# A token shift made tile by tile, context sums moved forward, and expert blocks split among the gather's copies

## The chip, the cores and the metric

The kernel runs on one core of a Trainium2 chip. Its time is the device time of one execution in microseconds (us), and the metric is the median of several runs. TensorE is PE in the profile, VectorE is DVE, ScalarE is ACT, GpSimd is POOL and SyncE is SP.

## The reference

256 tokens of width 1024 pass through two blocks of two layers each. The first block has a pooling and neighbourhood-attention layer and then an RWKV layer; it also carries a context sequence of 256 tokens (CTX) beside the latent one (X). The second block has a differential and a sparse attention layer, each followed by a mixture of 16 experts in 4 groups. The parts that matter here:

```python
def centred_shift(x):
    prev = jnp.pad(x[:, :-1], ((0, 0), (1, 0), (0, 0)))
    nxt = jnp.pad(x[:, 1:], ((0, 0), (0, 1), (0, 0)))
    return 0.5 * (prev + nxt) - x

xx = centred_shift(h)
mix = lambda j: h + xx * mu[j]
r = mix(0) @ wr        # latent tokens only
k = mix(2) @ wk        # context and latent tokens; also w, v, a, g from mixes 1, 3, 4, 5
```

The shift pads with a zero token at either end, so the sum at an edge is the one neighbour there is, which the program copies. In an expert layer each token takes one group of four experts by its router logits, and in it the two best experts with weights from the logits. An expert computes `(silu(x @ w_gate) * (x @ w_up)) @ w_down`.

## The kernel before

**Order.** Each engine has one program written out by hand, and it runs in that order. `step(...)` raises a semaphore and may name an event; `after(event)` gives the value to wait for. Tiles hold 128 features by 256 tokens, so the width of 1024 is eight tiles, k = 0 to 7. All 318 weight blocks (1 MB each) come through a ring of four slots (`N_SLOTS`), in the order of use. SP issues block j when block j - 4 is marked "used". `take_bank` hands out the PSUM banks in turn from a given list, and PE waits there until the last holder's result is taken.

**Mixes** (`mixes_vector`, from line 1784; `features_tensor`, 1882; `features_scalar`, 1944). ACT adds the shift of the modulation to the eight tiles of X (`shifted_scalar`, line 855). DVE then runs `shifted(X)`: the sum of both neighbours for all tiles (L1791), two edge copies (L1792, L1793), and 0.5 x sum - h (L1795). The mixes of `r` follow, one per k (L1804). PE multiplies them by wr, tile by tile (g = 0 to 7, each over all k, L941, two tiles per weight block). Behind g = 3 come the sums of squares of the context (L787), for which DVE and ACT have meanwhile finished the context's residual; and then g = 4 to 7. The root of these sums (L811) releases DVE's reciprocal (L818) and scaling (L847), ACT's shift (L855), `shifted(CTX)` and the mixes of `k` over both sequences. In between ACT splits the wk weights into high parts (`wk_high`, L1715) and DVE into low parts (L1720), and ACT copies wr's results out (L1395), tile 7 only after it has rounded all mixes of `k` (`mix_k_high`, L1726). `wk_tensor` (L1744) takes three banks for its first three tiles and walks k over them. Products whose result nobody reads (`unread_products`, L798) fill PE's time ahead of waits: 12 before wr and 3 before wk.

**Experts** (`moe_tensor`, 2857; `moe_vector`, 3018; `moe_scalar`, 3173; both layers). The router's products and transposes are followed by a gather: one-hot matrices times tokens give the inputs of five windows of 128 slots. The eight `pair` products (windows 0 and 1) and the eight times two `rest` products (windows 2 to 4) are copied out of their banks by ACT and DVE (L3184, L3188, L3094, L3098). Then weight block 0 is split into a high part on ACT (`Splits.high`, L507) and a low part on DVE (`Splits.low`, L516), and so on. There are 20 units; unit u does `gate_up(u)` (24 products of 512 columns, L2933 to L2935), `turn(u)` (two transposes, L2946) and `down(u)` (12 products, L2964 to L2966). Units 0 and 1 use the same weights on windows 0 and 1. `gate_up(u + 1)` is issued ahead of `down(u)`, with `turn(u)` between its two halves. Between unit 0's gate_up and unit 1's, PE transposes the places (L2996) and sums the slot weights (L3003, 10 products of 4 columns, 20 records), which wait for the token weights that DVE works out (L3110 to L3118).

## Time and profile before

| | |
|---|---|
| median of 3 runs | 2454.49 us (2449.64 to 2457.53) |
| the profiled execution | 2451.6 us, its span 2449.8 us |
| busy: PE, DVE, ACT | 94%, 69%, 41% of the span |
| mean granted clock of TensorE | 0.976 of full speed |
| read from HBM | 343.96 MB, 141 GB/s over the span |

The span is from the first instruction to the last. A busy PE is one with a product in its pipeline. The idle time given with a row is that of its engine just before it, with the instruction that ended it. An fp32 product shows as two records, so "x24" of such products is 12 of them; products of rounded (fp32r) operands show as one.

### The profile page before, as it was taken

To read this page: it belongs to the slowest core of one execution; us is meant where nothing else is said; L and a number is where in the kernel's file an instruction comes from. 1 tells how busy PE (TensorE), PEld (TensorE's weight loads), DVE (VectorE), ACT (ScalarE), POOL (GpSimd) and SP (SyncE) were. 2 spreads that over 40 slices of the span, in tenths; PEclk is the share of its full clock that TensorE was granted. 3 is DMA by queue.
4 is the path that set the end of the run, shared out by engine and by line. 5 is a ranking of instruction groups with operands and counts; after the bars stand their busy time and mean duration, and the time that the engine had idled before them with its cause. 6 is when DMAs were issued, how large, how long until landed. Compare 5 with 4: busy or idle time off the path is not lost.

```text
span 2449.8 us, 46605 instructions
## 1 busy us (share of the span) xinstructions
PE 2294.3 (94%) x20260; PEld 1907.2 (78%) x20260; DVE 1698.9 (69%) x3082; ACT 1006.5 (41%) x1763; POOL 44.7 (2%) x53
## 2 busy tenths in 40 slices
PE   7988999999999999999999989998999999898997
PEld 6864578888868678998897789895677878676786
DVE  7988698867746367887763887765455866646576
ACT  2244242332323225544422553344345655544464
POOL 1000000000000000000000000020000011000000
PEclk9999999999999989999999999999989999998999
DMA  8512437656512000000003577540055853104484
GB/s 341 206 52 86 155 139 274 242 205 245 218 64 105 31 1 3 4 3 3 12 4 124 211 267 295 224 172 18 1 195 216 338 203 113 70 1 157 169 335 180
DMA packets 47308, 348.00 MB, mean 142 GB/s; under 512 B 5264, under 2 KB 5280, under 8 KB 5760
## 3 DMA queue, kind: packets, MB, share of 16 engines
q1 hardware_dynamic: 45936, 334.52, 36.7%
q0 software_dynamic: 1168, 10.51, 1.1%
q8 instruction: 159, 2.61, 0.4%
q14 instruction: 45, 0.37, 0.0%
HBM read 343.96 MB, written 1.05 MB: 141 GB/s over the span
## 4 chain that ended last, share of the span: by engine, by line
PE 75%; DVE 17%; ACT 6%; issue 1%; DMA 1%; DVEq 0%; ACTq 0%; POOLq 0%
PE banks L538 25%; PE banks L2071 7%; PE banks L941 6%; PE banks L2933 3%; PE banks L2934 3%; PE banks L2935 3%; PE banks L1930 2%; DVE arena L617 2%; PE banks L787 2%; PE banks L1744 2%; PE banks L636 2%; PE banks L2148 2%; PE banks L2964 2%; PE banks L2966 2%; PE banks L2965 2%
## 5 line engine op out<-in xcount | busy, mean ns | idle before, releaser
L617 DVE SCALAR_TENSOR_TENSOR arena<-weight_slots,silu_c,arena 128x256 f32<-128x256 f32 x776 | 314.9, 479 | 0.0
L516 DVE TENSOR_TENSOR moe_w_low<-weight_slots,moe_w_high 128x2048 fp32r<-128x2048 f32 x96 | 217.9, 2288 | 69.0 <-ACT moe_w_high L507 68.1
L507 ACT ACTIVATE mlp_w_high<-weight_slots 128x2048 fp32r<-128x2048 f32 x64 | 122.3, 1911 | 180.8 <-PE banks L538 115.6
L507 ACT ACTIVATE moe_w_high<-weight_slots 128x2048 fp32r<-128x2048 f32 x96 | 181.1, 1910 | 22.9 <-PE banks L2966 19.7
L516 DVE TENSOR_TENSOR mlp_w_low<-weight_slots,mlp_w_high 128x2048 fp32r<-128x2048 f32 x64 | 146.4, 2287 | 48.7 <-ACT mlp_w_high L507 48.6
L941 PE MATMUL banks<-arena,weight_slots 128*128 128x256 f32 (+1 forms) x640 | 171.9, 425 | 2.8 <-DVE arena L1804 1.4
L2071 PE MATMUL banks<-weight_slots,arena 64*64 64x64 f32 (+1 forms) x3648 | 147.0, 223 | 18.9 <-ACT arena L2091 13.3
L2071 PEld LDWEIGHTS banks<-weight_slots,arena 64*64 64x64 f32 x3648 | 138.9, 134 | 27.2 <-ACT arena L2091 15.2
L941 PEld LDWEIGHTS banks<-arena,weight_slots 128*128 128x128 f32 x640 | 122.0, 192 | 47.0 <-issue 33.6
L2933 PE MATMUL banks<-moe_w_high,slots_x 128*128 128x512 f32 x320 | 131.9, 412 | 3.2 <-DVE moe_w_low L516 3.2
L2934 PE MATMUL banks<-moe_w_low,slots_x 128*128 128x512 f32 x320 | 128.2, 401 | 0.0
L2935 PE MATMUL banks<-moe_w_high,slots_x 128*128 128x512 f32 x320 | 128.1, 400 | 0.0
L2299 ACT ACTIVATE weight_slots<-banks 128x512 f32<-128x512 f32 x80 | 46.9, 595 | 120.0 <-DVE weight_slots L2478 94.1
L2148 PE MATMUL banks<-weight_slots 64*64 64x64 f32 x2560 | 83.6, 220 | 9.2 <-DVE weight_slots L2515 9.2
L2148 PEld LDWEIGHTS banks<-weight_slots 64*64 64x64 f32 x2560 | 78.9, 135 | 11.2 <-DVE weight_slots L2515 11.2
L2515 DVE TENSOR_TENSOR weight_slots<-banks,constants 128x512 f32<-128x512 f32 x80 | 54.2, 688 | 40.4 <-PE banks L2071 40.4
L614 DVE TENSOR_SCALAR arena<-weight_slots,silu_c 128x256 f32<-128x256 f32 x184 | 56.2, 348 | 32.9 <-PE banks L636 19.1
L1181 ACT ACTIVATE arena<-arena 128x256 f32<-128x256 f32 (+2 forms) x128 | 62.2, 488 | 36.7 <-DVE arena L1125 36.5
L2071 PE MATMUL banks<-arena 64*64 64x64 f32 (+1 forms) x1600 | 77.1, 226 | 0.0
L787 PE MATMUL banks<-arena,constants 128*128 128x256 f32 (+1 forms) x224 | 69.2, 435 | 6.4 <-ACT arena L839 6.4
L2933 PEld LDWEIGHTS banks<-moe_w_high,slots_x 128*128 128x128 f32 x320 | 61.3, 191 | 17.9 <-DVE moe_w_low L516 4.2
L2071 PEld LDWEIGHTS banks<-arena 64*64 64x64 f32 x1600 | 74.1, 134 | 0.3 <-issue 0.3
(428 smaller groups left out, 5109.3 us busy)
## 6 DMA issues: line engine op xcount, KB each, us to landing
weight_slots<-weights SPq DMA_DIRECT2D x318, 1024.0 KB, 4.8
arena<-small POOLq DMA_DIRECT2D x1, 2560.0 KB, 9.0
arena<-x_t POOLq DMA_DIRECT2D x1, 2048.0 KB, 9.6
arena<-bias POOLq DMA_DIRECT2D x1, 2048.0 KB, 8.4
constants<-consts POOLq DMA_DIRECT2D x1, 1410.0 KB, 14.6
out_t<-arena SPq DMA_DIRECT2D x1, 1024.0 KB, 3.9
parameters<-params POOLq DMA_DIRECT2D x1, 763.0 KB, 18.4
arena<-pool_inv POOLq DMA_DIRECT2D x1, 512.0 KB, 9.6
```

What stands on the lines that cost most here:

```text
L507: nc.scalar.activation(self.pair(j)[0], slot(j, 0, SLOT), ACT.Copy).then_inc(*act.step("high", j))
L516: nc.vector.tensor_tensor(self.pair(j)[1], slot(j, 0, SLOT), self.pair(j)[0], ALU.subtract).then_inc(*v.step("used", j))
L538: ins = nc.tensor.matmul(out, self.pair(j)[part][:, at:at + P], x(k), start=start and n == 0 and k == 0, stop=stop and n == 2 and k == til ...
L617: nc.vector.scalar_tensor_tensor(a_, w, c, a_, ALU.mult, ALU.add).then_inc(*v.step())
L787: ins = nc.tensor.matmul(psum(SUMS_BANK[segs[-1]], 0, len(segs) * SEQ), cn("ones"), squares_of(key, segs, k), start=(k == 0), stop=(k == K ...
L941: ins = nc.tensor.matmul(psum(b, 0, w), slot(j, k, 256, i * P, P), moving(k), start=(k == 0), stop=(k == KT - 1))
L1181: nc.scalar.activation(S[:, u % N, c:c + w], S[:, u % N, c:c + w], ACT.Exp, bias=M[:, u % N, 3 + j:4 + j], accum_out=M[:, u % N, 6 + j:7 + ...
L2071: ins = nc.tensor.matmul(psum(b, n * width, width, r), lhs, rhs, start=(i == 0), stop=(i == len(ts) - 1))
L2148: ins = nc.tensor.matmul(psum(b, p * 64, 64, r), Z[r, p, :], XI[r, p, :], start=False, stop=True, skip_group_check=True)
L2933: nc.tensor.matmul(psum(b), x_hi, wh, start=(k == 0), stop=False)
L2934: nc.tensor.matmul(psum(b), x_hi, wl, start=False, stop=False)
L2935: ins = nc.tensor.matmul(psum(b), x_lo, wh, start=False, stop=(k == KT - 1))
```

## The change

The diff changes three things. The token shift and the first mix that needs it are made tile by tile, in a pipeline on DVE over three tiles. PE's first four wr tiles advance together, k by k, and the context's sums follow them; 8 unread products stand before wr where there were 12. In both expert layers the gather's banks are fixed in an order (`GATHER_BANKS`), blocks 0 and 1 are split among the copies of the rest, the five unread products ahead of the first unit go, the slot weights are summed between the two halves of the second unit, and the places are transposed behind it; ACT copies them behind that unit's SiLU. Blocks 2 and 3 are split at other places of the same lists too.

```diff
--- before.py
+++ after.py
@@ -1785,24 +1785,41 @@
 
...
 
-            def shifted(seg):
-                v.wait_ge(*after("h", "n1_1", KT - 1, seg))
-                H, S = HT[:, seg], XX[:, seg]
-                nc.vector.tensor_tensor(S[:, :, 1:255], H[:, :, 0:254], H[:, :, 2:256], ALU.add).then_inc(*v.step())
-                nc.vector.tensor_copy(S[:, :, 0:1], H[:, :, 1:2]).then_inc(*v.step())
-                nc.vector.tensor_copy(S[:, :, 255:256], H[:, :, 254:255]).then_inc(*v.step())
-                v.wait_ge(*v.own)
-                nc.vector.scalar_tensor_tensor(S, S, 0.5, H, ALU.mult, ALU.subtract).then_inc(*v.step())
-                v.wait_ge(*v.own)
-
-            shifted(X)
+            def mixed_tile(i, k):
+                n, mu, segs = MIX_ORDER[i]
+                sg = seg_of(segs)
+                nc.vector.scalar_tensor_tensor(MIX[i % 2][:, sg, k, :], XX[:, sg, k, :],
+                                               pr("mu", mu * KT + k, 1), HT[:, sg, k, :], ALU.mult, ALU.add).then_inc(*v.step("mix", n, k))
+
+            def shifted_and_mixed(seg, i):
+
+                summed, centred = {}, {}
+                for k in range(KT + 2):
+                    if k < KT:
+                        v.wait_ge(*after("h", "n1_1", k, seg))
+                        H, S = HT[:, seg, k, :], XX[:, seg, k, :]
+                        nc.vector.tensor_tensor(S[:, 1:255], H[:, 0:254], H[:, 2:256], ALU.add).then_inc(*v.step())
+                        nc.vector.tensor_copy(S[:, 0:256:255], H[:, 1:255:253]).then_inc(*v.step())
+                        summed[k] = v.own
+                    if 1 <= k <= KT:
+                        v.wait_ge(*summed[k - 1])
+                        S = XX[:, seg, k - 1, :]
+                        nc.vector.scalar_tensor_tensor(S, S, 0.5, HT[:, seg, k - 1, :], ALU.mult, ALU.subtract).then_inc(*v.step())
+                        centred[k - 1] = v.own
+                    if k >= 2:
+                        v.wait_ge(*centred[k - 2])
+                        mixed_tile(i, k - 2)
+
             for i, (n, mu, segs) in enumerate(MIX_ORDER):
...
                     v.wait_ge(*after(*MIX_END[MIX_ORDER[i - 2][0]]))
-                sg = seg_of(segs)
-                for k in range(KT):
-                    nc.vector.scalar_tensor_tensor(MIX[i % 2][:, sg, k, :], XX[:, sg, k, :],
-                                                   pr("mu", mu * KT + k, 1), HT[:, sg, k, :], ALU.mult, ALU.add).then_inc(*v.step("mix", n, k))
+                if n == "r":
+                    shifted_and_mixed(X, i)
+                elif n == "k":
+                    shifted_and_mixed(CTX, i)
+                else:
+                    for k in range(KT):
+                        mixed_tile(i, k)
                 if n == "r":
...
                     inverse_root_vector(v, "y_x02", CTX)
@@ -1812,7 +1829,6 @@
                     inverse_root_vector(v, "n1_1", CTX)
...
                     v.stage("mixes")
-                    shifted(CTX)
                 if n == "k":
...
                     mix_k_low(v)
@@ -1881,12 +1897,38 @@
 
...
             mv = lambda i, segs: (lambda k: MIX[i % 2][:, seg_of(segs), k, :])
-            def context_sums(g):
-                if g == 3:
-                    x_sums_tensor(pe, "n1_1", [CTX])
-                    pe.stage("project_wr")
-            project_tensor(pe, "wr", "wr", lambda k: MIX[0][:, X, k, :], lambda k: [("mix", "r", k)], [X], "project_wr",
-                           [0, 1, 2, 3, 4, 6], context_sums)
+            pe.stage("project_wr")
+            WR_BANKS, blocks = [0, 1, 2, 3, 4, 6], {}
+
+            def wr_part(g, k):
+                return nc.tensor.matmul(psum(bank_of(("wr", g)), 0, SEQ), slot(blocks[g // 2], k, 256, g % 2 * P, P),
+                                        MIX[0][:, X, k, :], start=(k == 0), stop=(k == KT - 1))
+
+            def wr_done(ins, g):
+                ins.then_inc(*pe.step("wr", g))
+                if g % 2:
+                    pe.mark("used", blocks[g // 2])
+
+
+            for n in range(2):
+                blocks[n] = next_block(pe, "wr")
+            for g in range(4):
+                take_bank(pe, ("wr", g), WR_BANKS)
+            for k in range(KT):
+                pe.wait_ge(*after("mix", "r", k))
+                for g in range(4):
+                    ins = wr_part(g, k)
+                    if k == KT - 1:
+                        wr_done(ins, g)
+            x_sums_tensor(pe, "n1_1", [CTX])
+            pe.stage("project_wr")
+            for g in range(4, KT):
+                if g % 2 == 0:
+                    blocks[g // 2] = next_block(pe, "wr")
+                take_bank(pe, ("wr", g), WR_BANKS)
+                for k in range(KT):
+                    ins = wr_part(g, k)
+                wr_done(ins, g)
             wk_tensor(pe)
...
                 pe.stage("low_rank")
@@ -2854,6 +2896,8 @@
         def y_banks(w):
...
 
+        GATHER_BANKS = [6, 7, 4, 5, 0, 2, 1, 3]
+
         def moe_tensor(pe, l):
...
             start = block_of[f"moe{l}"][0]
@@ -2895,7 +2939,7 @@
 
...
             for k in range(KT):
-                b = take_bank(pe, ("pair", l, k), range(8))
+                b = take_bank(pe, ("pair", l, k), [GATHER_BANKS[k]])
                 for part in range(2):
...
                         pe.wait_ge(*after("token_low", l, 2 * t + k // 4))
@@ -2905,7 +2949,7 @@
             pe.wait_ge(*after("places", l, 1))
...
                 for part in range(2):
-                    b = take_bank(pe, ("rest", l, k, part), range(8))
+                    b = take_bank(pe, ("rest", l, k, part), [GATHER_BANKS[(2 * k + part) % 8]])
                     for t in range(2):
...
                                                PLACES_R[:, t, SEQ:WINDOWS * P], start=(t == 0), stop=(t == 1))
@@ -2987,24 +3031,31 @@
                 if w < WINDOWS - 1:
...
 
-            unread_products(pe, 5, bank_state["next"] % 8)
+            def slot_weights():
+                b = take_bank(pe, ("slot_weights", l), range(6))
+                pe.wait_ge(*after("token_weights", l))
+                for w in range(WINDOWS):
+                    for t in range(2):
+                        ins = nc.tensor.matmul(psum(b, 4 * w, 4), PLACES[:, t, w * P:(w + 1) * P], ROUTE["first"][:, t],
+                                               start=(t == 0), stop=(t == 1))
+                ins.then_inc(*pe.step("slot_weights", l))
+
+            def places_turned():
+                for n in range(3):
+                    b = take_bank(pe, ("places_t", l, n), range(4))
+                    for w in range(2 * n, min(2 * n + 2, WINDOWS)):
+                        for t in range(2):
+                            ins = nc.tensor.transpose(psum(b, (w % 2) * SEQ + t * P, P), PLACES[:, t, w * P:(w + 1) * P],
+                                                      cn("ident"))
+                    ins.then_inc(*pe.step("places_t", l, n))
+
             gate_up(0)
-            for n in range(3):
...
-            ins.then_inc(*pe.step("slot_weights", l))
             for u in range(N_UNITS):
-                if u + 1 < N_UNITS:
+                if u == 0:
+                    gate_up(1, slot_weights)
+                    turn(0)
+                    places_turned()
+                elif u + 1 < N_UNITS:
                     gate_up(u + 1, lambda: turn(u))
...
                     turn(u)
@@ -3097,15 +3148,14 @@
                 v.wait_ge(*after("rest", l, k, 1))
...
                     *v.step("taken", "rest", l, k, 1))
-            MOE[l].low(v, 0)
-            MOE[l].low(v, 1)
+                if k in (1, 4):
+                    MOE[l].low(v, k // 4)
 
...
             tt(R["less2"], R["max2"], R["max1"], ALU.subtract).then_inc(*v.step("top_less", l))
-            MOE[l].low(v, 2)
             v.wait_ge(*after("route_exp", l))
...
             step(nc.vector.reciprocal(R["sum"], R["sum"]))
@@ -3116,6 +3166,7 @@
             step(tt(R["first"], R["first"], four(R["w1"]), ALU.mult))
...
             tt(R["first"], R["first"], R["second"], ALU.add).then_inc(*v.step("token_weights", l))
+            MOE[l].low(v, 2)
             MOE[l].low(v, 3)
...
             nc.vector.tensor_copy(R["weights"], psum(bank_of(("slot_weights", l)), 0, 4 * WINDOWS).rearrange(
@@ -3183,23 +3234,19 @@
                 act.wait_ge(*after("pair", l, k))
...
                                      ACT.Copy).then_inc(*act.step("taken", "pair", l, k))
+            MOE[l].high(act, 0)
             for k in range(KT):
...
                     *act.step("taken", "rest", l, k, 0))
+                if k == 4:
+                    MOE[l].high(act, 1)
             act.wait_ge(*after("group_less", l))
             nc.scalar.activation(R["less"], R["less"], ACT.Exp).then_inc(*act.step())
-            MOE[l].high(act, 0)
-            MOE[l].high(act, 1)
+            MOE[l].high(act, 2)
             act.wait_ge(*after("top_less", l))
             nc.scalar.activation(R["less2"], R["less2"], ACT.Exp).then_inc(*act.step("route_exp", l))
-            MOE[l].high(act, 2)
             load_table(act, ACT.Silu)
-            for n in range(3):
-                act.wait_ge(*after("places_t", l, n))
...
             MOE[l].high(act, 3)
...
             act.stage(f"experts{l}")
@@ -3219,6 +3266,12 @@
                 if u >= 3:
...
                 nc.scalar.activation(SG[:, u % 3], psum(b, 0, SEQ), ACT.Silu).then_inc(*act.step("silu", l, u))
+                if u == 1:
+                    for n in range(3):
+                        act.wait_ge(*after("places_t", l, n))
+                        m = min(2, WINDOWS - 2 * n)
+                        nc.scalar.activation(PLACES_T[:, 2 * n:2 * n + m, :], psum(bank_of(("places_t", l, n)), 0, m * SEQ).rearrange(
+                            "p (a b) -> p a b", b=SEQ), ACT.Copy).then_inc(*act.step("taken", "places_t", l, n))
                 for i in early:
...
                 for y in range(WINDOWS):
@@ -3603,7 +3656,7 @@
             unread_products(pe, 1, 0)
...
             x_sums_tensor(pe, "n1_1", ONE, 5)
-            unread_products(pe, 12, 0)
+            unread_products(pe, 8, 0)
             features_tensor(pe)
...
             readout_tensor(pe)
```

## Rows read from the trace of the kernel before

**Rows 1.** The page: busy shares, the chain by engine, the weight transfers.
```profile
PE 2294.3 (94%) x20260; PEld 1907.2 (78%) x20260; DVE 1698.9 (69%) x3082; ACT 1006.5 (41%) x1763; POOL 44.7 (2%) x53
...
PE 75%; DVE 17%; ACT 6%; issue 1%; DMA 1%; DVEq 0%; ACTq 0%; POOLq 0%
...
weight_slots<-weights SPq DMA_DIRECT2D x318, 1024.0 KB, 4.8
```

**Rows 2.** The chain in order of time, 690 to 860: start, us, what.
```profile
722.77 2.30 DVE arena L1795
...
725.73 14.05 PE banks L941 x64
739.78 3.47 PE banks L787 x16
...
743.27 0.48 ACT arena L811
...
754.22 5.40 DVE arena L1804 x8
...
760.27 0.28 ACT arena L1395
...
760.69 44.38 PE banks L1744 x192
```

**Rows 3.** Timeline of DVE, 700 to 790: start, us, instruction, idle before.
```profile
720.30 2.28 DVE L1791 TENSOR_TENSOR arena<-arena 128x2032 f32<-128x2032 f32 x1 [0.66 <-ACT arena L855]
722.50 0.17 DVE L1792 COPY arena<-arena 128x8 f32<-128x8 f32 x1
...
725.10 3.25 DVE L1804 SCALAR_TENSOR_TENSOR arena<-arena,parameters 128x256 f32<-128x256 f32 x8
```

**Rows 4.** Timeline of PE, 700 to 790.
```profile
713.83 10.46 PE L798 MATMUL banks<-constants 128*128 128x512 f32 x24
...
756.89 2.74 PE L798 MATMUL banks<-constants 128*128 128x512 f32 x6
```

**Rows 5.** Timeline of ACT, 700 to 790.
```profile
737.60 2.00 ACT L1715 ACTIVATE wk_w_high<-weight_slots 128x1024 fp32r<-128x1024 f32 x2 [0.89 <-DMA weight_slots<-weights]
```

**Rows 6.** Timeline of PE, 356 to 380.
```profile
368.77 1.40 PE L538 MATMUL banks<-quarter_low,mlp_w_high 128*128 128x512 f32 x2 [4.84 <-DVE quarter_low L1589]
369.97 2.98 PE L538 MATMUL banks<-quarter_high,mlp_w_high 128*128 128x512 f32 x8
372.78 1.98 PE L538 MATMUL banks<-quarter_high,mlp_w_low 128*128 128x512 f32 x8
```

**Rows 7.** Windows of 2 us: stretch, busy by engine, PEclk, DMA share, GB/s.
```profile
370.00:372.00 2.00, 2.00 (x6) 1.63 (x5) 2.00 (x6) 1.20 (x1) 0.00 (x0) 0.50 0.98 401
```

**Rows 8.** Timeline of PE, 1740 to 1840.
```profile
1787.88 4.45 PE L798 MATMUL banks<-constants 128*128 128x512 f32 x10
...
1802.87 4.43 PE L3003 MATMUL banks<-arena,places 128*128 128x4 f32 x20 [3.42 <-DVE arena L3118]
1807.16 0.77 PE L2933 MATMUL banks<-moe_w_high,slots_x 128*128 128x512 f32 x1
```

**Rows 9.** Windows of 4 us, 1808 to 1816.
```profile
1808.00:1812.00 4.00, 4.00 (x11) 3.03 (x11) 0.10 (x1) 0.00 (x0) 0.00 (x0) 0.50 0.51 215
1812.00:1816.00 4.00, 4.00 (x19) 3.16 (x18) 1.35 (x2) 2.52 (x4) 0.00 (x0) 0.94 0.00 0
```

**Rows 10.** Timeline of ACT, 1740 to 1840.
```profile
1788.21 3.70 ACT L507 ACTIVATE moe_w_high<-weight_slots 128x2048 fp32r<-128x2048 f32 x2
```

**Rows 11.** Timeline of DVE, 1740 to 1840.
```profile
1783.22 5.42 DVE L3098 CAST slots_x<-banks 128x384 fp32r<-128x384 f32 x8
1790.15 4.49 DVE L516 TENSOR_TENSOR moe_w_low<-weight_slots,moe_w_high 128x2048 fp32r<-128x2048 f32 x2 [1.51 <-ACT moe_w_high L507]
...
1796.62 0.15 DVE L3107 TENSOR_TENSOR arena<-arena 128x2 f32<-128x2 f32 x1
```

**Rows 12.** Timeline of SP's queue, 1740 to 1840.
```profile
1775.05 63.42 SPq L432 DMA_DIRECT2D weight_slots<-weights  x13
```

15 lines of the change are left out of this document (removed).

## The prediction

> **What bounds the kernel now.** I began with the page. The busy shares say that TensorE (PE) works in 94% of the span, and the chain that ended last runs through PE for 75% and through VectorE (DVE) for 17% [rows 1]. A single change elsewhere therefore only counts where PE waits, works on something unneeded, or runs at half clock. The diff touches two kinds of places, so I read the chain and the timelines there, and then the windows for the granted clock.
>
> In the mixes, PE waits for the first product of wr. DVE forms the centred shift of all eight tiles in one piece (2.28 us and 2.30 us), and only then the first mix, so PE starts at 725.73 [rows 2, 3]. The 12 unread products (24 records, 10.46 us) before it are cover for that wait [rows 4]. Later the chain leaves PE for the context half: root at 743.27 on ScalarE (ACT), then DVE to 759.62, ACT's rounding of the last mix, ACT's copy of wr's tile 7 at 760.27, and PE's first wk product at 760.69 [rows 2]. The reader is to see that PE isn't the bound at this place: its wr work ended near 757, and three unread products fill the hole [rows 4].
>
> In each expert layer PE first does five unread products (4.45 us), since the first weight block is split only after the gather's copies: ACT from 1788.21, DVE from 1790.15 [rows 8, 10, 11]. Then, after the first unit, it waits 3.42 us for the token weights, works 4.43 us on slot weights, and the next 512-column products run 0.63 us each instead of the 0.39 of full clock [rows 8]. The clock was 0.50 in 1808 to 1812, that is 1.2 GHz, and its mean of 0.94 in the next four puts the return to 2.4 GHz at 1812.5 [rows 9].
>
> **The mixes, step by step.** Per tile the new loop issues a sum of 254 columns (2.28/8 = 0.29, with its start about 0.34), an edge copy (0.17 long, about 0.07 between starts), a centring (0.40) and a mix (0.40 at 256 columns) [rows 3]: 1.2 us. DVE is free at 719.64 (its first sum starts at 720.30 after 0.66 idle). The first mix comes after three sums and copies, two centrings and itself: 3 x 0.41 + 2 x 0.40 + 0.48 = 2.5, so at 722.1. PE starts at 722.2, which is 3.5 us earlier. It needs 14.05/8 = 1.76 us per k [rows 2], more than DVE's 1.2, so it isn't starved. The 8 unread products that remain take 2/3 of 10.46 us and end at 720.9.
>
> DVE ends this loop at 729.2, 0.9 us later than now. The context squares come that much later, and the other wr tiles cover it: PE reaches the context sums at 736.3 and their last at 739.4, the last square is there at 737.1. So wr ends 3.2 us earlier, at 753.9.
>
> This gain doesn't reach wk. First, wr's block 0 now stays in use until k = 7 of tile 1, about 735.4 and not 732.8, since four tiles advance together. A transfer takes 4.8 us from issue [rows 1], so wk's first block lands at 740.2; ACT waits for it today until 737.60 [rows 5]. Behind that wait on ACT are two roundings (2.0 us), two copies and the root of the context sums, at 742.8. The 3.4 us gained by the sums shrink to some 0.4 us. Second, the context loop on DVE costs per tile 0.34 + 0.07 + 0.40 + 0.67 = 1.48 [rows 2, 3], together 11.8 us from the last scaled tile. Now it is 10.8: the first mix at 754.22, less the two large steps, the copies and the same 0.6 of waiting for ACT, puts that tile's end at 748.8, and the last mix ends at 759.6. ACT rounds the last mix, copies wr tile 7, and the third wk tile takes the bank of just that tile. So PE starts wk at 760.69 + 0.9 - 0.35 = 761.3: 0.6 us later. The bounds are -1.0 (if the root is as early as its sums allow and no start is longer) and +1.5.
>
> Third, PE is now idle from 756.6 to 761.3, 4.7 us instead of 1.1. The nearest row is the wait of 4.84 us at 368.77: the first eight products behind it took 2.98 us and the next eight 1.98, at a clock of 0.50 in between, and the two just behind the wait 1.40 [rows 6, 7]. That is 1.0 + 0.5 = 1.5 us; the bounds are 0 (no drop) and 2.6 (as long as the low stretch after the slot weights). I take 1.5. Mixes together: **+2.1 us**. Nothing behind covers it, for PE runs through wk without a wait.
>
> The Trainium skill, "TensorE: Matmul & The Clock Gate", section "Why this matters for your kernels", warns of just such an idle gap between bursts of products, after which the engine is back at half clock. By it the 1.5 us are due; without it the mixes cost 0.6 us. The trace agrees at 368.77.
>
> **An expert layer.** ACT's splitting of block 0 moves ahead of the rest's copies. The block is issued at 1775.05 [rows 12] and lands at 1779.8, so it is no wait: ACT splits at 1782.6 to 1784.5, DVE forms the low part at 1784.5 to 1786.75 (4.49 for two, [rows 11]). DVE's copies of tiles 2 to 4 are queued behind it; PE needs the bank of tile 2's second part at 1786.8 and gets it at 1787.3. ACT's own delay of 1.9 us is covered by its four banks. The gather stretches by 0.5 us (bounds 0 and 2). New banks spare the first gathers a wait for token copies: -0.25. The unread products go: -4.45, and the first unit starts at 1788.4. Its second half needs block 1: ACT 1786.3 to 1788.2, DVE to 1790.5, while PE comes there at 1791.2. Covered.
>
> DVE then copies three rests (5.42/8 is a pace set by PE; alone about 0.47 each), ends them at 1792.0, and needs 2.2 us to the step at 1796.62 of today (12 steps from 1794.6, 0.18 each [rows 11]), so 1794.2; ACT's exponential and nine such steps give token weights at 1796.2. PE is halfway through the second unit at 1796.9, so the wait of 3.42 goes whole; its slack is 0.7 us. The slot weights (4.43) and the transposes cost what they cost, only elsewhere. The transposes' copies on ACT (three, 1.3 us) go behind the second unit's SiLU, where ACT waits for PE anyway, and PE needs them only eight units later.
>
> The clock: today 12 products start at 1807.16 at 1.2 GHz and take 5.1 us (0.427 for 512 columns), where at full clock eight take 1.98 [rows 6] and 12 take 2.9: 2.2 us lost [rows 8, 9]. PE was busy with the 4-column products for 4.43 us, and the clock was still low behind them, so 4.4 us of them between two dense halves may well lower it. The nearest rows are again those at 368.77: I put 1.3 us, bounds 0 and 2.4. Per layer: -4.45 + 0.5 - 0.25 - 3.4 - 2.2 + 1.3 = **-8.5 us**, -17.0 for both; the second layer adds -0.5, since its first gather waits longer for a bank today. Later units move as a whole: PE is their bound, and each split is released by PE's own progress.
>
> Sum: 2.1 - 17.5 = -15.4 us. Against the profiled execution (2451.6 us, span 2449.8) it gives 2436.2; against the median of the three runs, 2454.5, it gives 2439.1. I say **2438.5 us**.
>
> **Rivals.**
> *The clock holds.* The slot weights count as work and wk's gap falls well: then -17.5 - 2.6 - 1.5 = -21.6, 2433. For it: PE issues the slot weights without a pause, unlike in the wait of rows 6; against it: [rows 6, 7, 9]. Chance 0.16.
> *The weight stream takes the lead back.* The first transfer of a layer is issued at 1775.05 either way [rows 12], so if transfers and splits set the end of the layer, both leads are lost and only the mixes' +2.1 stays: 2456.6, no change. For it: a block costs DVE 2.25 us and ACT 1.85 of their time; against it: the chain hardly leaves PE. Chance 0.10.
> *A late token weight.* DVE's chain has 0.7 us of slack; 2 to 3 us more cost 2 per layer, with the clock 4: -8, 2446. Chance 0.10.
> *Slower.* The clock stays at 1.2 GHz behind the slot weights. A product costs 0.19 us more there; to turn -15.4 into +7.4 it takes 120 products, over three units, some 25 us of low clock in each layer. Against it: the clock was back after 3 to 5 us of dense work in both stretches [rows 6, 9]. Chance 0.03, 2462.
> The forecast, -11 to -20, has 0.61.
>
> **Numbers.** The measurement can tell about 0.3% (7.4 us) from no change. Faster by more: 0.61 + 0.16 + most of the late-weight case = 0.86; within: 0.10; slower: 0.04. The range takes in the clock rival below and the late-weight case above: 2431 to 2447.
>
> **What would show it.** PE's first wr product 3.5 us earlier against the norm before it, but its first wk product no earlier, behind a gap of 4 to 5 us and with a half-clock stretch after it. In each layer no unread products behind the gather, no wait at line 3003's place, the first down product some 10 us earlier than now, less what the clock takes. The prediction is wrong if wk starts 2 us earlier, if the gather stretches by more than 2 us, or if later units show new waits for low parts.

## The result and the profile after

| | before | after |
|---|---|---|
| median of 4 runs | 2453.02 us (2449.64 to 2457.53) | 2426.36 us (2423.67 to 2428.44) |
| ratio | | 0.9894, interval 0.9879 to 0.9909 |
| the profiled execution | 2451.6 us, span 2449.8 us | 2424.98 us, span 2423.1 us |
| mean granted clock of TensorE | 0.976 | 0.981 |

The kernel is faster by 26.7 us. The forecast was 15.4, and the time lies below the predicted range of 2431 to 2447 us. The page of the changed kernel, in the rows that answer to [rows 1]:

```profile
PE 2272.6 (94%) x20232; PEld 1894.0 (78%) x20232; DVE 1699.0 (70%) x3122; ACT 1004.0 (41%) x1763; POOL 43.8 (2%) x53
...
PE 76%; DVE 16%; ACT 5%; issue 1%; DMA 1%; DVEq 0%; ACTq 0%; POOLq 0%
...
weight_slots<-weights SPq DMA_DIRECT2D x318, 1024.0 KB, 4.9
```

PE's busy time fell by 21.7 us, but only 28 of its 20260 records went, 20 of them the unread products of the two expert layers (8.9 us) and 8 those ahead of wr (10.46 - 7.03 = 3.4 us). For the other 9.4 us PE must run faster somewhere. The mean clock says how much. A mean of 0.976 over 2449.8 us is 118 us at 1.2 GHz (twice 0.024 of the span), and 0.981 over 2423.1 is 92. Some 26 us less at half speed are up to 13 us of time (what falls into a wait costs nothing), so up to half of the gain. This is the first thing to look for in the stretches.

**The mixes.** First the chain in order of time, 690 to 860 (start, us, what), against [rows 2]:

```profile
728.29 13.20 PE banks L1904 x60
741.51 4.79 DMA weight_slots<-weights
746.32 1.07 ACT wk_w_high L1715
...
747.41 2.36 DVE wk_w_low L1720 x2
...
751.47 3.26 DVE arena L847 x8
...
765.96 0.63 ACT mix_k_high L1726
767.00 45.98 PE banks L1744 x192
```

PE's timeline in this stretch, against [rows 4]:

```profile
720.04 7.03 PE L798 MATMUL banks<-constants 128*128 128x512 f32 x16
728.29 14.05 PE L1904 MATMUL banks<-arena,weight_slots 128*128 128x256 f32 x64 [1.21 <-DVE arena L1791]
...
759.44 2.74 PE L798 MATMUL banks<-constants 128*128 128x512 f32 x6
767.00 7.30 PE L1744 MATMUL banks<-mix_k_high,wk_w_high 128*128 128x512 f32 x24 [4.82 <-ACT arena L1395]
```

Absolute times of the two traces don't compare: at the 700 us mark the changed one is already 6.2 us late, in code that the change doesn't touch (10.2 us more of it ran at half clock, which is 5.1 us). So I count from the first unread product ahead of wr. wr starts 8.25 us behind it, where it was 11.90 (725.73 - 713.83): 3.6 us earlier. wk starts 46.96 us behind it, where it was 46.86. The lead is gone, and the chain shows where: it now runs through the transfer of wk's first block, issued at 741.51, ACT's rounding of it at 746.32, and DVE's low parts of it, which hold DVE until 749.77. The reciprocal of the context's root stands behind them. The idle gap before wk is 4.82 us long, and the first 24 wk products take 7.30 us instead of 5.70. The windows of 2 us say why (stretch, busy by engine, PEclk, DMA share, GB/s):

```profile
768.00:770.00 2.00, 2.00 (x6) 1.54 (x5) 2.00 (x5) 0.00 (x0) 0.00 (x0) 0.50 0.00 0
770.00:772.00 2.00, 2.00 (x8) 1.61 (x8) 2.00 (x5) 0.00 (x0) 0.00 (x0) 0.80 0.00 0
```

**The expert layer.** PE's timeline in layer 0, 1764 to 1812, against [rows 8]:

```profile
1781.95 0.35 PE L2946 MATMUL banks<-places,token_high 128*128 128x256 f32 x1 [1.30 <-DVE token_low L3139]
...
1791.23 0.61 PE L2954 MATMUL banks<-places,token_low 128*128 128x384 f32 x2 [0.29 <-DVE slots_x L3149]
...
1792.39 0.39 PE L2977 MATMUL banks<-moe_w_high,slots_x 128*128 128x512 f32 x1
...
1800.79 2.29 PE L3039 MATMUL banks<-arena,places 128*128 128x4 f32 x20
...
1806.04 1.25 PE L3048 MATMUL banks<-constants,places 128*128 128x128 f32 x10
1807.22 0.48 PE L3008 MATMUL banks<-moe_w_high,hidden_t_high 128*128 128x512 f32 x1
```

There are no unread products and no wait, as predicted. But the slot weights, the same 20 records of 4 columns, take 2.29 us, and they took 4.43 [rows 8]. The windows of 4 us of the kernel before show what they ran in:

```profile
1796.00:1800.00 4.00, 3.44 (x21) 2.70 (x19) 1.82 (x6) 3.17 (x3) 0.00 (x0) 1.00 0.82 338
1800.00:1804.00 4.00, 1.13 (x6) 1.13 (x6) 3.13 (x11) 3.64 (x7) 0.00 (x0) 0.78 0.36 111
1804.00:1808.00 4.00, 4.00 (x18) 3.90 (x19) 2.27 (x3) 0.00 (x0) 0.00 (x0) 0.50 0.59 201
```

and of the changed one:

```profile
1800.00:1804.00 4.00, 4.00 (x30) 3.64 (x29) 4.00 (x2) 1.75 (x2) 0.00 (x0) 1.00 0.13 20
1804.00:1808.00 4.00, 4.00 (x25) 3.31 (x23) 1.36 (x4) 1.76 (x2) 0.00 (x0) 1.00 0.99 397
1808.00:1812.00 4.00, 4.00 (x19) 3.23 (x18) 2.90 (x3) 3.75 (x6) 0.00 (x0) 1.00 0.33 115
```

Before, the clock fell inside the wait: a mean of 0.78 over 1800 to 1804 means 1.8 us at half speed, so from 1802.2. The slot weights began at 1802.87 and ran at 1.2 GHz from end to end. The 12 products behind them (L2933 to L2935) took 5.26 us, from 1807.16 [rows 8] to the next transposes,

```profile
1812.42 0.40 PE L2946 MATMUL banks<-constants,arena 128*128 128x128 f32 x2
```

and in the changed kernel 12 such products take 2.80 us (1797.99 to 1800.79). In these windows of the changed kernel the clock doesn't fall at all. The token weights, the other point at risk, are done at 1799.97 in DVE's timeline, 0.8 us before PE reaches the slot weights:

```profile
1799.80 0.17 DVE L3168 TENSOR_TENSOR arena<-arena 128x8 f32<-128x8 f32 x1
```

Counted from the first unread product behind the router's input (L798 at 1761.15 before, 1766.96 after; in layer 1 at 2204.57 and 2193.91), the steps of a layer stand so:

| us behind that point | layer 0 before | after | layer 1 before | after |
|---|---|---|---|---|
| end of the gather | 26.73 | 25.43 | 27.09 | 25.38 |
| first product of unit 0 | 31.34 | 25.43 | 31.79 | 25.38 |
| slot weights | 41.72 | 33.83 | 42.08 | 33.77 |
| first down product | 54.31 | 40.26 | 54.64 | 40.13 |

So the first down product comes 14.05 and 14.51 us earlier. Each layer has three later waits, of 1.4, 0.9 and 2.0 us in both traces, and at the last of them the lead is still 14.0 and 14.4 us. Behind it the trace of before has another half-clock stretch in both layers and the changed one has none, which adds 0.6 us to each lead; the change doesn't touch this place, so I leave that out of the layers' sum. Together: +6.2 before the mixes, +1.7 in them, -2.1 from there to the router of layer 0, -14.0, -2.5 from there to the router of layer 1, -14.4 and -1.5 behind them make -26.6, the difference of the two profiled executions.

### The profile page after: what moved, and what is told of

The parts are those of the page before. It is cut to its first block, busy times and chain, and to the rows that moved or that the text cites. A ratio compares the mean times of both kernels' runs of the same rounds, so it can differ in the third digit from the quotient of the medians.

```text
span 2423.1 us, 46590 instructions
## 1 busy us (share of the span) xinstructions
PE 2272.6 (94%) x20232; PEld 1894.0 (78%) x20232; DVE 1699.0 (70%) x3122; ACT 1004.0 (41%) x1763; POOL 43.8 (2%) x53
## 4 chain that ended last, share of the span: by engine, by line
PE 76%; DVE 16%; ACT 5%; issue 1%; DMA 1%; DVEq 0%; ACTq 0%; POOLq 0%
PE banks L538 25%; PE banks L2113 7%; PE banks L941 6%; PE banks L2977 3%; PE banks L2978 3%; PE banks L2979 3%; PE banks L1972 2%; DVE arena L617 2%; PE banks L1744 2%; PE banks L636 2%; PE banks L787 2%; PE banks L3008 2%; PE banks L2190 2%; PE banks L3010 2%; PE banks L3009 2%
## 5 line engine op out<-in xcount | busy, mean ns | idle before, releaser
L941 PE MATMUL banks<-arena,weight_slots 128*128 128x256 f32 (+1 forms) x512 | 144.5, 439 | 1.4 <-ACT arena L1206 1.4
L941 PEld LDWEIGHTS banks<-arena,weight_slots 128*128 128x128 f32 x512 | 98.4, 193 | 41.5 <-issue 31.3
L538 PE MATMUL banks<-quarter_high,mlp_w_high 128*128 128x512 f32 x256 | 69.4, 409 | 3.3 <-ACT quarter_high L1565 3.2
## 6 DMA issues: line engine op xcount, KB each, us to landing
constants<-consts POOLq DMA_DIRECT2D x1, 1410.0 KB, 14.7
```

The lines of the kernel that those rows point to most:

```text
L538: ins = nc.tensor.matmul(out, self.pair(j)[part][:, at:at + P], x(k), start=start and n == 0 and k == 0, stop=stop and n == 2 and k == til ...
L941: ins = nc.tensor.matmul(psum(b, 0, w), slot(j, k, 256, i * P, P), moving(k), start=(k == 0), stop=(k == KT - 1))
```

## The experiments

Each kernel ran on one chip beside the kernel before, whose median was 2451.7 us (17 runs) for the first four, 2452.2 (15 runs) for the next four, and 2454.2 (11 runs) for the last four. "The changed kernel" is the one of the diff. The ratios are always to the kernel before on the same chip. A difference to the changed kernel is one of medians taken at different times, beside kernels before whose medians lie up to 2.5 us apart, so 2 or 3 us of it say nothing.

**The mixes alone** (mixes_only): the change without its edits of the expert layers.

```diff
-            shifted(X)
             for i, (n, mu, segs) in enumerate(MIX_ORDER):
...
+                if n == "r":
+                    shifted_and_mixed(X, i)
+                elif n == "k":
+                    shifted_and_mixed(CTX, i)
...
-            unread_products(pe, 12, 0)
+            unread_products(pe, 8, 0)
```

> The kernel before with the token shift, the wr order and the 8 unread products alone; the expert layers as before. My theory: the mixes cost 1.5 to 2 us (wk's first product no earlier, then a half-clock stretch of 1.6 us), so the ratio is 1.000 to 1.001 and the whole gain lies in the expert layers. Rival: part of the 26.7 us comes from the mixes, then 3 us or more faster than before, ratio below 0.9985.

Measured: 2451.05 us (11 runs), ratio 1.000 [0.9991, 1.0008]. PE's timeline:

```profile
714.14 7.03 PE L798 MATMUL banks<-constants 128*128 128x512 f32 x16
722.38 14.05 PE L1904 MATMUL banks<-arena,weight_slots 128*128 128x256 f32 x64 [1.21 <-DVE arena L1791]
```

wr starts 8.24 us behind the unread products, and wk 47.03 us behind them, after a wait of 4.90. The interval allows 2 us of gain or of loss; the trace has 1.8 us of loss, 0.2 for the later start of wk and 1.6 for its first 24 products, which take 7.34 us. The tile by tile mixes alone win nothing.

This trace also shows the old expert layers a second time. In layer 0 the same slot weights behind the same wait took less than in the trace of before:

```profile
1800.71 2.83 PE L3045 MATMUL banks<-arena,places 128*128 128x4 f32 x20 [3.41 <-DVE arena L3160]
```

Here the clock fell 1.8 us after the first of them (0.81 over 1800 to 1804), and not inside the wait. In layer 1 they took 4.43 us again. So the old order always ends in low clock, but where it falls differs between executions.

**The expert layers alone** (experts_only): the changed kernel with the old mixes.

```diff
-                if n == "r":
-                    shifted_and_mixed(X, i)
-                elif n == "k":
-                    shifted_and_mixed(CTX, i)
...
+            shifted(X)
...
-            unread_products(pe, 8, 0)
+            unread_products(pe, 12, 0)
```

> The kernel before with the edits in the expert layers alone. My theory: the two layers give 14 us each less what free-running clock drops take, so 2424 to 2427 us, ratio 0.988 to 0.990, at or slightly below the changed kernel. Rival (the gain needs both parts): above 2432 us.

Measured: 2422.98 us (4 runs), ratio 0.9885 [0.9871, 0.9900]. That is -28.7 us, some 14.4 for each layer. The slot weights take 2.29 us in both layers. The whole gain is in the expert layers. The median is 3.4 us below the changed kernel's, which fits the 1.7 us that the mixes lose there, but the intervals overlap.

**Only the slot weights and the transposes moved** (slots_moved): the kernel before with the slot weights between the halves of the second unit, the transposes and their copies on ACT behind it, and the low part of block 2 behind the token weights. The unread products, the banks and the splits of blocks 0 and 1 stay.

```diff
             for u in range(N_UNITS):
-                if u + 1 < N_UNITS:
+                if u == 0:
+                    gate_up(1, slot_weights)
+                    turn(0)
+                    places_turned()
+                elif u + 1 < N_UNITS:
                     gate_up(u + 1, lambda: turn(u))
...
-            MOE[l].low(v, 2)
...
             tt(R["first"], R["first"], R["second"], ALU.add).then_inc(*v.step("token_weights", l))
+            MOE[l].low(v, 2)
```

> The kernel before with only the slot weights put between the halves of the second unit and the places transposed behind it (with their ACT copies); the splits, the banks and the five unread products as before. My theory: this takes the wait of 3.4 us, the slot weights' slow 2.1 us and the half-clock stretch of 2.2 us behind them, 7.5 to 8 us in each layer, 15 to 16 in all, 2437 to 2438 us; the slot weights run in 2.3 us. Rival (the move only shifts the wait, as token weights are late): the wait reappears in the second unit and at most 4 us per layer are won.

Measured: 2437.69 us (6 runs), ratio 0.9945 [0.9933, 0.9958], -14.0 us. PE's timeline and the windows of 4 us:

```profile
1804.34 2.29 PE L2997 MATMUL banks<-arena,places 128*128 128x4 f32 x20
1806.49 0.48 PE L2935 MATMUL banks<-moe_w_high,slots_x 128*128 128x512 f32 x1
```

```profile
1804.00:1808.00 4.00, 4.00 (x30) 3.63 (x29) 2.87 (x3) 1.75 (x2) 0.00 (x0) 1.00 0.60 168
```

This one move gives half of the gain. By the prediction it was worth its wait and the old dip less a new one, 3.4 + 2.2 - 1.3 = 4.3 for each layer. It gave 7.0. The wait (3.4), the slot weights' own time (2.1) and the old dip (2.5 as measured) sum to 8.0, for a layer in which the clock falls inside the wait; where it falls later, their own time is 0.5 to 1.1 (mixes_only, banks_only).

**The splits early, the slot weights before unit 1** (splits_early): the changed kernel with the old mixes, and the places and the slot weights between unit 0 and unit 1, where the kernel before has them; their bank is one of two that the transposes don't use.

```diff
             gate_up(0)
+            places_turned()
+            slot_weights()
             for u in range(N_UNITS):
-                if u == 0:
-                    gate_up(1, slot_weights)
-                    turn(0)
-                    places_turned()
-                elif u + 1 < N_UNITS:
+                if u + 1 < N_UNITS:
```

> The expert edits without the move of the slot weights: blocks 0 and 1 split among the copies, fixed banks, no unread products, but places transposed and slot weights summed ahead of the second unit, as before (the slot weights in one of two banks that the places don't use). My theory: 4.5 us of unread products less 0.6 of stretched gather are won in front, but PE then arrives at the token weights earlier: they come at 1799.9 on the clock of the changed kernel and PE at about 1799.4, so the wait is below 1 us, the clock need not fall, and most of the gain is there: 10 to 13 us per layer, 2428 to 2434 us. Rival: both parts are independent and this one gives only the 4 us per layer of the unread products, 2445 us.

Measured: 2431.73 us (5 runs), ratio 0.9916 [0.9904, 0.9929], -20.0 us. PE's timeline in layer 0:

```profile
1795.78 1.26 PE L3006 MATMUL banks<-constants,places 128*128 128x128 f32 x10
1797.80 2.50 PE L2997 MATMUL banks<-arena,places 128*128 128x4 f32 x20 [0.77 <-DVE arena L3124]
1800.16 0.78 PE L2935 MATMUL banks<-moe_w_high,slots_x 128*128 128x512 f32 x1
1800.73 0.63 PE L2936 MATMUL banks<-moe_w_low,slots_x 128*128 128x512 f32 x1
```

The move and the splits overlap: 14.0 and 20.0 us alone, 28.7 together. With the splits early, the token weights come early too, and 0.77 us of the wait is left. Even so the clock falls in both layers. In layer 0 it falls in the last of the slot weights (they take 2.50 us and the products behind them 0.63 each, to 1803.3), in layer 1 sooner, and they take 3.10. So at that place, with the transposes and a short wait ahead, it is lost without a long hole.

**The slot weights three times** (slots_x3): the changed kernel, with the same ten products issued three times over.

```diff
-                for w in range(WINDOWS):
+                for w in [w for _ in range(3) for w in range(WINDOWS)]:
                     for t in range(2):
```

> The changed kernel with the products of the slot weights done three times over (same result, 6.8 us of 4-column products in each layer in place of 2.3). My theory: 2.3 us between two dense halves is too short to lower the clock, but 6.8 us is long enough: the clock falls inside, the later ones take 0.22 us each, so 4.6 us plus 1 to 2 us of slow products plus up to 2 us of slow dense work behind, 6 to 8 us per layer, 12 to 16 us slower than the changed kernel. Rival (4-column products count as work for the clock): 9.2 us slower and a clock of 1.00 throughout.

Measured: 2442.08 us (8 runs), ratio 0.9954 [0.9939, 0.9968], 15.7 us over the changed kernel (14.7 by the ratios). PE's timeline and the windows of layer 0:

```profile
1803.11 8.83 PE L3039 MATMUL banks<-arena,places 128*128 128x4 f32 x60
1811.80 0.77 PE L2977 MATMUL banks<-moe_w_high,slots_x 128*128 128x512 f32 x1
```

```profile
1806.00:1808.00 2.00, 2.00 (x18) 2.00 (x17) 0.69 (x1) 0.00 (x0) 0.00 (x0) 0.86 0.80 315
1808.00:1812.00 4.00, 4.00 (x20) 4.00 (x21) 0.02 (x1) 0.00 (x0) 0.00 (x0) 0.50 0.84 350
```

The clock does fall under 4-column products, 4.3 us after the first of them here (0.86 over 1806 to 1808), and stays low for 10.2 us. So the prediction's "may well lower it" was right of 4.4 us and more of such products. The rival that they count as dense work, with a clock of 1.00 throughout, is refuted. Of 2.29 us of them the forecast was mostly wrong; whole_ctx below shows the exception.

**The unread products kept** (unread_kept): the changed kernel, with five unread products ahead of the first unit.

```diff
+            unread_products(pe, 5, bank_state["next"] % 8)
             gate_up(0)
```

> The changed kernel with the five unread products put back ahead of the first unit. My theory: they lie on PE's path with nothing to cover, 4.4 us in each layer, 8.8 us slower than the changed kernel, 2435 us. Rival: they keep the clock up or only shift a wait for block 1 or the token weights, then under 3 us per layer.

Measured: 2433.88 us (4 runs), ratio 0.9921 [0.9895, 0.9946], 7.5 us over the changed kernel by the medians and 6.6 by the ratios, whose intervals overlap. The trace is clearer. The products take 4.45 and 4.56 us, and the first down product comes 4.3 us later than in the changed kernel in layer 0 and 6.8 us later in layer 1. There PE also waits 0.73 us for a bank ahead of them, and the clock falls at the end of the slot weights (0.89 over 2236 to 2240, 0.68 over the next four). At the last wait of each layer PE is still 4.3 and 6.8 us later. So their removal is paid out in time, and no late split takes it back.

**The gap before wk filled** (gap_filled): the changed kernel with eight unread products for three.

```diff
             pe.stage("project_wk")
-            unread_products(pe, 3, 5)
+            unread_products(pe, 8, 5)
```

> The changed kernel with 8 unread products ahead of wk where it has 3 (5 more, 4.4 us, in a hole of 4.8 us). My theory: wk's first product starts no later, the first 24 products take 5.7 us and not 7.3, so 1.6 us faster than the changed kernel, ratio to before 0.9885 (changed: 0.9894). Rival: the hole isn't what lowers the clock, and nothing changes.

Measured: 2419.72 us (5 runs), ratio 0.9867 [0.9846, 0.9887]. PE's timeline:

```profile
763.81 7.03 PE L798 MATMUL banks<-constants 128*128 128x512 f32 x16
771.35 5.70 PE L1744 MATMUL banks<-mix_k_high,wk_w_high 128*128 128x512 f32 x24 [0.52 <-ACT arena L1395]
```

wk starts 46.94 us behind the unread products ahead of wr, as in the changed kernel, but its first 24 products take 5.70 us and not 7.30. The gap costs 1.6 us, then, for the clock. The medians differ by 6.6 us; the intervals of the ratios overlap, and I take no more than the 1.6 as shown (0.52 us of waiting is left in the gap).

**The root first** (root_first): ACT takes the root of the context's sums ahead of wk's first roundings, with the copies and roundings that stood before it put behind; DVE's low parts of wk go behind the mixes of `k`.

```diff
-            rw_out(act, "wr", range(2), act_copy)
-            wk_high(act, [0, 1])
-            rw_out(act, "wr", range(2, 4), act_copy)
+            rw_out(act, "wr", range(4), act_copy)
             root_scalar(act, "n1_1", CTX)
             shifted_scalar(act, "n1_1", 1, 0, CTX)
-            wk_high(act, [2])
+            wk_high(act, [0, 1, 2])
```

> The changed kernel with ACT taking the root of the context sums before it rounds wk's first weights (whose block lands late), and DVE making the low parts of wk's first three tiles after the mixes of k. My theory: the root comes at 0.1 us behind the context sums, 3 us earlier, so the mixes of k and wk's first product come 3 us earlier and the hole before wk is 1.8 us, with less or no slow clock: 3 to 4.6 us faster than the changed kernel, ratio 0.9875 to 0.988. Rival: the context loop on DVE itself (11.7 us) or the later low parts bound wk, and nothing or less than 1 us is won.

Measured: 2423.94 us (6 runs), ratio 0.9884 [0.9865, 0.9902]. ACT's timeline, then PE's:

```profile
747.43 0.47 ACT L811 ACTIVATE arena<-banks,constants 128x256 f32<-128x256 f32 x1 [1.98 <-PE banks L787]
```

```profile
765.27 5.70 PE L1744 MATMUL banks<-mix_k_high,wk_w_high 128*128 128x512 f32 x24 [1.49 <-ACT arena L1395]
```

The root is now released by the sums. wk starts 43.62 us behind the unread products, 3.3 earlier, and the clock holds. So it was the queues of ACT and DVE, splitting a block that lands late ahead of the root and its reciprocal, that swallowed the 3.6 us gained at wr. The run moves both and doesn't tell them apart. Its median is 2.4 us below the changed kernel's, with overlapping intervals; the 3.3 us and the 1.6 of the clock are read from the trace.

**The last copy early** (copy_early): root_first, and ACT copies wr's tile 7 between the roundings of k = 5 and 6 instead of behind all of them.

```diff
                 nc.scalar.activation(K_HI[:, :, k, :], MIX[1][:, :, k, :], ACT.Copy).then_inc(*act.step("mix_k_high", k))
+                if k == 5:
+                    rw_out(act, "wr", [KT - 1], act_copy)
...
             mix_k_high(act)
-            rw_out(act, "wr", [KT - 1], act_copy)
```

> root_first, and in it ACT copies wr's last tile out after rounding mix 5 of k, not after mix 7. My theory: the third wk tile's bank is what holds PE once the mixes come tile by tile; with it free at 5 of 8, PE starts wk some 1.5 us earlier and follows the mixes, so its first 24 products end about 1.5 us earlier than in root_first against the same norm before wr; ratio 0.9875 to 0.988. Rival: PE, starting early, only waits inside the 24 products for the last mixes, and their end doesn't move (under 0.5 us).

Measured: 2416.55 us (5 runs, 2414.89 to 2424.61), ratio 0.9845 [0.9830, 0.9859]. PE's timeline:

```profile
721.69 7.03 PE L798 MATMUL banks<-constants 128*128 128x512 f32 x16
...
761.08 2.74 PE L798 MATMUL banks<-constants 128*128 128x512 f32 x6
763.65 5.70 PE L1746 MATMUL banks<-mix_k_high,wk_w_high 128*128 128x512 f32 x24
```

wk starts 41.96 us behind the unread products, 5.0 earlier than in the changed kernel, with no wait and no low clock: 6.6 us in this stretch. The ratio is below the changed kernel's by 0.0049, and their intervals don't touch. The medians differ by 9.8 us, so 3 us of that lie outside this stretch and aren't explained. This is the version that beats both kernels.

**The context's shift in one piece** (whole_ctx): root_first with the sum, the edges and the centring of the context in one instruction each again, the latent half tile by tile.

```diff
                 elif n == "k":
-                    shifted_and_mixed(CTX, i)
...
+                    nc.vector.tensor_tensor(S[:, :, 1:255], H[:, :, 0:254], H[:, :, 2:256], ALU.add).then_inc(*v.step())
...
+                    for k in range(KT):
+                        mixed_tile(i, k)
```

> root_first with the context's shift made for all eight tiles in one piece, as in the kernel before (X stays tile by tile). My theory: wk waits for the end of DVE's context loop, whatever its first mix does, and eight short sums, copies and centrings cost DVE 0.9 us more than one large piece less the 0.6 us of waiting for ACT; so wk's first product comes 0.9 us earlier than in root_first. Rival: it comes later, by the pipeline's head start of some 3 us.

Measured: 2421.62 us in one run. wk starts 43.20 us behind the unread products, 0.4 earlier than in root_first, where 0.9 was expected. In layer 0 this trace has what the prediction feared: the slot weights end at 1800.4 after 2.29 us, and 1.3 us later the clock falls inside the dense products behind them.

```profile
1798.14 2.29 PE L3045 MATMUL banks<-arena,places 128*128 128x4 f32 x20
...
1801.81 0.63 PE L2983 MATMUL banks<-moe_w_high,slots_x 128*128 128x512 f32 x1
```

It stays low for 3.4 us (0.71 over 1800 to 1804, 0.86 over the next four), and the first down product comes 1.5 us later than in the changed kernel. Of the nine traces in which the slot weights stand once between the halves of the second unit, this layer and layer 1 of unread_kept have such a dip; the other 16 layers have none.

**All three** (all_three): copy_early with the context's shift in one piece (the diffs of the last two together).

> root_first with both: wr's last tile copied early and the context's shift in one piece. My theory: the best of the versions, first 24 wk products ending 2 us earlier than in root_first; 2420 to 2423 us. Rival: the early copy is of use only with tile-by-tile mixes, and the two don't add.

Measured: 2416.82 us (5 runs), ratio 0.9844 [0.9830, 0.9858]; wk starts at 41.88. It adds nothing to copy_early, in which wk waits for nothing.

**The gather's banks alone** (banks_only): the kernel before with the fixed order of banks.

```diff
-                b = take_bank(pe, ("pair", l, k), range(8))
+                b = take_bank(pe, ("pair", l, k), [GATHER_BANKS[k]])
```

> The kernel before with only the gather's banks in the fixed order. My theory: in the second expert layer the first gather starts 1.2 us earlier behind a wait of 1.3 and not 2.5 us, in the first layer the third pair 0.3 us earlier; the rest is as before and the time 1 us less, within what one run can tell. Rival: the fixed order makes a later gather wait.

Measured: 2451.1 us in one run, which says nothing of 2 or 3 us. In the trace the first gather of layer 1 stands behind a wait of 1.29 us; before it was 2.50. The eight pairs take 4.08 us in both layers, counted from the first product to the start of the last two. Before they took 5.94 and 5.14, and the windows of the kernel before show the clock low in them (of banks_only it is 1.00 there throughout):

```profile
1780.00:1784.00 4.00, 4.00 (x24) 4.00 (x24) 2.32 (x5) 2.12 (x4) 0.00 (x0) 0.78 1.00 424
2220.00:2224.00 4.00, 3.30 (x20) 3.33 (x21) 3.22 (x5) 1.20 (x2) 0.00 (x0) 0.76 0.98 414
```

The slot weights, unchanged in this run, take 3.42 and 3.10 us behind waits of 3.51 and 3.33: the clock falls after they have begun, as in layer 0 of mixes_only.

## Why the prediction was wrong

The direction, the places and the waits that would go were right. The sum for an expert layer was -8.5 (and -9.0 for the second), and the runs show -14.0 and -14.4.

**The step that failed** is "The slot weights (4.43) and the transposes cost what they cost, only elsewhere", and with it the term +1.3 for a new dip. The 4.43 us was read as the price of 20 such records. It was their price at 1.2 GHz, as the windows of the kernel before show: in that trace the clock had fallen at 1802.2, inside the wait that the change removes. At 2.4 GHz they cost 2.29 us (in both layers of all nine traces in which they are issued once, between the halves of the second unit). I saw the low clock behind them [rows 9] and took the products for its cause, though it had fallen before the first of them. From there the second mistake followed: a time of 4.4 us of such work would have lowered the clock (slots_x3: after 4.3 us), but 2.29 us left it alone in 16 of 18 layers, the changed kernel's two among them. In the other two it cost 1.5 us, so the size of the term was right and its likelihood wrong. The two are 2.1 + 1.3 = 3.4 us for each layer.

How much of this a given execution pays differs. In three of the six old layers traced (before, mixes_only, banks_only) the clock fell only after the first slot weights, and they took 2.83 to 3.42 us. The trace of before has the dear case in both layers. In the trace of before the transposes and the wait were enough, since the clock fell ahead of the first slot weight. Where it fell later, the share of the wait and that of the small products stay open: splits_early cut the wait to 0.77 us and still lost it.

**Mis-sized:** the old dip, at 2.2. The 12 products took 5.26 us and not 5.1, and at full clock take 2.80 and not 2.9, which makes 2.5.

**Mis-sized:** the gather. Its stretch of 0.5 us for the early split is there (0.29 of wait and a slower pair of copies in the trace), but against it stood -0.25, or -0.75 in the second layer, for the banks, and the end of the gather came 1.3 and 1.7 us earlier. The pairs took 5.94 and 5.14 us, partly at half clock, and take 4.07 to 4.09 in both layers of all eleven traces with fixed banks. In layer 1 the wait of 2.50 us ahead of it, now 1.30, goes with the fall: with the old banks mixes_only and slots_moved have both again. In layer 0 the wait was 1.30 either way, and mixes_only and slots_moved, with the old banks, took 4.43 and 4.44 there. Why the clock fell there in the trace of before stays open, and 1.5 us of its 14.05 may be no merit of the change. Another 0.2 us in each layer is the low-part wait ahead of unit 0 (0.16 and 0.25), which went with the unread products.

**The terms of a layer against the table:** the unread products -4.45 (with that wait, -4.6 and -4.7), the wait -3.4 (gone), the old dip -2.2 (-2.5), the slot weights 0 (-2.1), the new dip +1.3 (none), the gather +0.25 (-1.3 and -1.7). The measured ones make -13.9 and -14.4, and the first down product came 14.05 and 14.5 earlier.

**The mixes** were right in size and nearly so in mechanism: +2.1 expected, of it 0.6 for a later start of wk and 1.5 for the clock; the traces show +0.1 and +1.6. wk's first block is issued at 741.51 and lands 4.8 us later, and ACT's roundings and the root stand behind it (root_first takes that away, and 3.3 us come back). Tile 7's copy holds the bank (copy_early, another 1.7). The prediction left out DVE's low parts of wk, which stand ahead of the root's reciprocal: the root came 0.7 us earlier and the scaling behind it only 0.3. Off by 0.5 us was the context loop: 1.40 us a tile, not 1.48, since two neighbouring steps overlap more.

The Trainium skill, "TensorE: Matmul & The Clock Gate", section "Why this matters for your kernels", warns of idle gaps of this length ahead of a burst. The gap of 4.82 us agrees, and gap_filled shows its price. But splits_early lost the clock with a wait of only 0.77 us, which is well below the gaps that it warns of; here a run of small products stood on both sides of it, and the measurement decides.

**The rivals.** "The clock holds" came true in the expert layers and not before wk. Its 2433 would have been 2434.5 with the mixes' dip; it lacked the slot weights' own time and the gather, as the forecast did. "The weight stream takes the lead back": refuted, the lead of 14.05 us at the first down product is 14.0 at the layer's last wait, and unread_kept loses what the products take. "A late token weight": it comes 0.8 us before PE needs it, where 0.7 was worked out. "Slower" rested on a clock that stays low behind the slot weights; only slots_x3 shows a long stretch of that.

The sum with the measured terms: +1.7 for the mixes, -28.4 for the layers, and +0.1 for code that the change doesn't touch, which is -26.6.

## What to carry to other kernels

Before a row's duration is carried to another place, look at the granted clock in which it was measured: work behind a long wait can have been timed at half speed, and a change that removes the wait gives that back too (here up to 4.6 us beside the 3.4 of the wait). Put the small products that wait for another engine inside a run of dense ones, late enough to wait for nothing, and keep them few: 20 records lost the clock in 2 of 18 layers, 60 in both of theirs. A start gained early in a stage is worth nothing until the queues of the next engines are put in the same order: here the places of a few copies, roundings and low parts on ACT and DVE held the 5 us.

## What the hardware showed unexpectedly

- A record of a 4-column product takes 0.11 us at 2.4 GHz (2.29/20) and 0.22 at 1.2 GHz (4.43/20). With so few columns I had thought it a fixed cost; it doubles at half the clock, and so nearly does the stretch of the weight loads beside it (2.43 and 4.34 us for the 20).
- Code that no edit touched differed by 6.2 us between the two traces by the 700 us mark, mostly since the clock fell at other places (5.1 us). In mixes_only the same slot weights took 2.83 us in one layer and 4.43 in the other, by where it fell. Five runs of gap_filled lie between 2419.2 and 2430.9. In such a kernel a gain of a few us is better read from one stretch of the trace than from a median.
- Very small work can lose the clock though PE never pauses: 2.29 us of 4-column products inside dense ones were followed by no dip in 16 of 18 layers and by one of 3.4 us in two. Three times as many (8.83 us as measured) cost 10.2 us at half speed.
